# RMS norms of a two-block transformer kernel: the row factor applied after the matrix products instead of before

## The reference

```python
def rms_norm(x, gain):
    y = x * lax.rsqrt(jnp.mean(x * x, axis=-1, keepdims=True) + RMS_EPS)
    return y * gain
# first stack, layer i
x = x + mixer(rms_norm(x, norm_mix[i]), ...)
x = x + memory_cross_attention(rms_norm(x, norm_mem[i]), rms_norm(mem, norm_mem_src[i]), ...)
x = x + swiglu(rms_norm(x, norm_ffn[i]), ffn_w_in[i], ffn_w_out[i])
# second stack, layer l
h = _rmsnorm(x, g_mix[l]);  proj = h @ w_in[l]
gates = jax.nn.sigmoid(gate_pre + gate_b[l])       # 4 x 1024 columns of proj
x = x + jnp.sum(gates * branch, axis=2) @ w_out[l]
h = _rmsnorm(x, g_ffn[l])
u = _depthwise_conv(h @ w_up, conv_w, conv_b)      # 3 taps along the sequence
gate, up = jnp.split(u, 2, axis=-1)
x = x + (jax.nn.silu(gate) * up) @ w_down
```

## Time and profile before

| what | value |
|---|---|
| median of three runs | 1889.57 us |
| span of the profiled execution | 1888.8 us |
| PE busy | 1749.1 us, 93% |
| DVE busy | 1123.0 us, 59% |
| ACT busy | 822.7 us, 44% |
| POOL busy | 372.9 us, 20% |
| DMA share of 16 engines | 45.9%, mean 143 GB/s |
| mean granted TensorE clock | 0.948 |

### The profile page before, as it was taken

The page is one execution under the profiler, slowest core; times in us unless marked ns, Lnnn a source line. Parts: engine busy times, 40 slices in busy tenths (PEclk is TensorE's granted clock), DMA queues, the critical chain, the costliest instruction groups (busy, mean ns, idle before and its releaser), DMA issues. The chain is left out here.

```text
span 1888.8 us, 27948 instructions
## 1 busy us (share of the span) xinstructions
PE 1749.1 (93%) x11243; PEld 1575.8 (83%) x11243; DVE 1123.0 (59%) x1644; ACT 822.7 (44%) x1207; POOL 372.9 (20%) x462
## 2 busy tenths in 40 slices
PE   7899789999998988999989999899997999989998
PEld 6767679987886777899878799799976889979996
DVE  5757655544544655555446775677734676667763
ACT  4333344433342433444334446356524434636652
POOL 1500100001430000000014871201101595211100
PEclk9978899999977998999999999999998999999999
DMA  6401256656420023565465333566545534256654
GB/s 244 163 24 56 71 157 180 187 181 193 160 90 12 12 92 87 148 186 184 169 187 169 122 130 117 145 170 179 184 137 172 178 118 146 104 151 182 187 187 155
DMA packets 298695, 269.89 MB, mean 143 GB/s; under 512 B 19008, under 2 KB 258624, under 8 KB 298560
## 3 DMA queue, kind: packets, MB, share of 16 engines
q1 hardware_dynamic: 298560, 268.05, 45.9%
HBM read 266.97 MB, written 1.05 MB: 142 GB/s over the span
## 5 line engine op out<-in xcount | busy, mean ns | idle before, releaser
L139 DVE TENSOR_TENSOR w_lo<-w_raw,w_hi 128x2048 fp32r<-128x2048 f32 (+1 forms) x257 | 567.5, 2210 | 322.6 <-ACT w_hi L138 321.2
L138 ACT ACTIVATE w_hi<-w_raw 128x2048 fp32r<-128x2048 f32 (+1 forms) x257 | 468.6, 1826 | 195.5 <-PE bank L421 180.7
L1401 PE MATMUL bank<-mf_h_hi,w_hi 128*128 128x256 f32 x704 | 199.4, 283 | 0.0
L1401 PE MATMUL bank<-cffn_h_hi,w_hi 128*128 128x256 f32 x704 | 199.4, 283 | 0.0
L1403 PE MATMUL bank<-mf_h_hi,w_lo 128*128 128x256 f32 x704 | 199.2, 283 | 0.0
L1403 PE MATMUL bank<-cffn_h_hi,w_lo 128*128 128x256 f32 x704 | 199.2, 283 | 0.0
L1402 PE MATMUL bank<-mf_h_lo,w_hi 128*128 128x256 f32 x704 | 199.2, 283 | 0.0
L1402 PE MATMUL bank<-cffn_h_lo,w_hi 128*128 128x256 f32 x704 | 199.2, 283 | 0.0
L1401 PE MATMUL bank<-mix_h_hi,w_hi 128*128 128x256 f32 x576 | 166.9, 290 | 0.0
L1402 PE MATMUL bank<-mix_h_lo,w_hi 128*128 128x256 f32 x576 | 163.9, 284 | 0.0
L1403 PE MATMUL bank<-mix_h_hi,w_lo 128*128 128x256 f32 x576 | 163.8, 284 | 0.0
(11 more groups left out here) (518 smaller groups left out, 3736.4 us busy)
## 6 DMA issues: line engine op xcount, KB each, us to landing
w_raw<-in_w_in SPq DMA_DIRECT2D x50, 1024.0 KB, 5.1
w_raw<-in_ffn_w_in SPq DMA_DIRECT2D x88, 512.0 KB, 5.2
w_raw<-in_w_up SPq DMA_DIRECT2D x88, 512.0 KB, 5.0
w_raw<-in_ffn_w_out SPq DMA_DIRECT2D x20, 1024.0 KB, 4.9
w_raw<-in_w_down SPq DMA_DIRECT2D x20, 1024.0 KB, 5.0
w_raw<-in_nsa_w_in SPq DMA_DIRECT2D x10, 1024.0 KB, 5.1
w_raw<-in_ab_w_in SPq DMA_DIRECT2D x8, 1024.0 KB, 8.0
w_raw<-in_mem_w_kv SPq DMA_DIRECT2D x8, 1024.0 KB, 5.3
```

Source lines behind the costliest of these rows:

```text
L138: return act.activation(hi, raw, ACT.Copy)
L139: return dve.tensor_tensor(self.lo[:, cut_slot, 0:k * n], raw, hi.bitcast(F32), ALU.subtract)
L1401: pe.matmul(out, h, hi[:, f, :], start=(f == 0), stop=False)
```

## The change

The factor 1/rms leaves the path to the first product. `Norm` is replaced by `Features`: plain PE transposes of raw rows (L242 of the changed kernel), ACT and DVE multiply by the gain alone and split. Three things follow.

1. **Turning inside the residual.** `Residual` now has chunks of two k-rows throughout. Its last two chunks are worked bank by bank, in the order (rows 0, columns 0), (rows 1, columns 0), (rows 0, columns 1), (rows 1, columns 1). After each bank DVE adds it to `x_rows`, and four transposes of that quarter stand in PE's list one bank later; the last quarter follows the last bank. ACT and DVE round and cut features 0 to 3 there; features 4 to 7 follow in the next body.
2. **The factor later.** Where rows are on partitions it is the scale of the copies out of PSUM. Where features are on partitions (`stationary_job`) a row of factors is needed along the free axis: `RowFactors` spreads, turns and copies it, PE doing its part after job 0. DVE then multiplies each bank by it. In `block_conv_ffn` this gives a buffer `before`, and the taps are computed from it, the side taps one round of the loop later on DVE; `wide_lo` moves to POOL. In `block_branches` DVE copies out the 16 gate jobs in place of ACT, and ACT adds the bias in the sigmoids, 32 of 256 columns instead of 8 of 1024.
3. **The ring.** The loop of the second stack now has two chunks less, and `w.skip` leaves slots out so that each round begins at the same place: one cut slot after gate job 7, one raw and one cut slot before the four `mix_chunks`. A chunk behind a skipped cut slot waits for a later chunk to be used than before.

```diff
+class Features:
+    def turn(self, pe, t, half):
+        for f in range(4 * half, 4 * half + 4):
+            ins = pe.transpose(self.view(f)[:, t * P:(t + 1) * P], self.src[:, t, f * P:(f + 1) * P],
+                               self.k.ident[:, :])
+        ins.then_inc(self.turned, 1)
+    def round(self, act, features):
+        for f in features:
+            if not self.first:
+                act.wait_ge(self.turned, 2 * (f // 4) + 2)
+            act.activation(self.hi[:, f, :], self.view(f), ACT.Copy, scale=self.gain[:, f:f + 1])\
+               .then_inc(self.hi_done, 1)
...
+class RowFactors:
+    def dve(self, dve):
+        self.features.wait_factor(dve)
+        dve.tensor_copy(self.wide.rearrange("p (t q) -> p t q", q=P), free(self.features.rstd, [[1, T], [0, P]]))\
+           .then_inc(self.spread, 1)
+    def pe(self, pe):
+        pe.wait_ge(self.spread, 1)
...
@@ class Residual
+    ORDER = [(0, 0), (1, 0), (0, 1), (1, 1)]
+    TAIL = 2
...
+        for i, (t, half) in enumerate(self.ORDER):
...
+            if i < 3:
+                ins.then_inc(self.summed, 1)
+            if i and self.then is not None:
+                self.turn(pe, i - 1)
+        if self.then is not None:
+            self.turn(pe, 3)
+
+    def turn(self, pe, i):
+        pe.wait_ge(self.added, i + 1)
+        self.then.turn(pe, *self.ORDER[i])
...
@@ class Weights, round_to
-            if c >= self.CUT:
-                act.wait_ge(self.used, c - self.CUT + 1)
+            before = self.last_in(self.cut_slot, self.cut_slot(c), c)
+            if before is not None:
+                act.wait_ge(self.used, before + 1)
...
@@ block_branches
-        gate_chunks = [w.add(stationary_chunk(a["w_in_2"][layer], 6656, (2 * P * j,), 2 * P)) for j in range(16)]
+        gate_chunks = [w.add(stationary_chunk(a["w_in_2"][layer], 6656, (2 * P * j,), 2 * P)) for j in range(8)]
+        w.skip(0, 1)
+        gate_chunks += [w.add(stationary_chunk(a["w_in_2"][layer], 6656, (2 * P * j,), 2 * P)) for j in range(8, 16)]
...
+        w.skip(1, 1)
         mix_chunks = [w.add(stationary_chunk(a["w_branch_2"][layer], D, (2 * P * j,), 2 * P)) for j in range(4)]
...
                     w.round_to(act, gate_chunks[AHEAD + i] + 2)
                     if i == 12:
-                        act.wait_ge(gated, 2 * (AHEAD + 11))
+                        act.wait_ge(gated, AHEAD + 11)
                         for j in range(OPEN):
                             open_gates(act, j)
-                    gate(act, AHEAD + i)
...
                 def step(dve, i):
+                    if i:
+                        gate(dve, AHEAD + i - 1)
                     make_masks(dve, i)
...
@@ block_conv_ffn, scalar
                 for j in range(KF + 2):
                     if j < KF:
                         w.round_to(act, up[j] + 2)
-                        act.wait_ge(w.used, up[j] + 1)
+                        act.wait_ge(scaled, j + 1)
                         if j >= 2:
                             act.wait_ge(prod, j - 1)
...
                     if 1 <= j <= KF:
                         act.wait_ge(sides, 4 * j)
@@ block_conv_ffn, vector
-                for j in range(KF + 2):
+                for j in range(KF + 1):
                     if j < KF:
                         w.cut_to(dve, up[j] + 2)
-                        dve.wait_ge(middle, 2 * j + 2)
+                        dve.wait_ge(w.used, up[j] + 1)
+                        if j == 0:
+                            dve.wait_ge(row_factors.done, 1)
+                        dve.tensor_tensor(before[:, j % 2, :, :], k.bank[j % 4][:, :].rearrange("p (a q) -> p a q", q=S),
+                                          free(row_factors.rows, [[0, 2], [1, S]]), ALU.mult).then_inc(scaled, 1)
+                    if j >= 1:
+                        i = j - 1
+                        dve.wait_ge(middle, 2 * i + 2)
                         for side in range(2):
                             for half in range(2):
...
+                                u, v = before[:, i % 2, half, :], conv[:, i % 2, half, :]
```

More of the change, by code:

```diff
@@ new lines, in turn_all, with square @@
+    def turn_all(self, pe):
+        for half in range(2):
+            for t in range(T):
+                self.turn(pe, t, half)
+    def square(self, act, t, part):
+        n = D // self.parts
+        act.activation(self.scratch[t * self.parts + part], self.src[:, t, part * n:(part + 1) * n], ACT.Square,
+                       accum_out=self.stat[:, part, t:t + 1]).then_inc(self.squares, 1)
+    def round(self, act, features):
[4 more added lines that the diff above has]
+               .then_inc(self.hi_done, 1)
@@ L443, in act @@
             w.round_following(act)
+        if self.then is not None:
+            for i in range(2):
+                act.wait_ge(self.added, i + 1)
+                self.then.square(act, i, 0)
+            self.then.round(act, range(4))
+            if not self.final:
+                self.then.round(act, range(4, KD))
+                for t in range(T):
+                    act.wait_ge(self.added, 3 + t)
+                    self.then.square(act, t, 1)
     def dve(self, dve):
@@ L1086, in _ @@
                 project.act(act, squares)
-                mem.norm.act_round(act)
+                mem.features.round(act, range(KD))
                 mem.act(act, 0)
@@ L1125, in _ @@
                 project.dve(dve, sums)
-                mem.norm.dve_cut(dve)
+                mem.features.cut(dve, range(KD))
                 mem.dve(dve, 0)
@@ L1586, in _ @@
             def _(act):
-                norm.act_square(act)
+                rows.round(act, range(4, KD))
+                for t in range(T):
+                    rows.square(act, t, 1)
                 w.round_to(act, 1)
-                norm.act_round(act)
-                mem.norm.act_square(act)
+                mem.act_square(act)
                 def squares(act, j):
@@ L2185, in _ @@
                 cut(dve, 1)
+                for j in range(AHEAD):
+                    gate(dve, j)
                 turn.dve(dve)
```

561 lines of the change are left out of this document (303 added, 258 removed).

## The result

The changed kernel takes 1952.4 us (median of four runs, 1950.4 to 1955.8), the kernel before 1889.3 us in runs on the same chip. The ratio is 1.033, 95% interval 1.031 to 1.036: 63 us slower. The forecast was 1911 us, in a range from 1884 to 1945.

A forecast was written before the change was run, and what follows sets the result against it. PE was taken as the busy engine, its largest waits at the norms' turning. Terms -74 - 1.5 + 12.6 + 60 + 24 = +21 us on 1888.8 gave 1910, as a median 1911 us; range 1884 to 1945.

The forecast's parts named there:

- Gaps at the norms: Nine PE stops for turning rows by scaled identities: 103.8 us before, each gap now 2.8 us, gaining 74 us.
- the loop's jump: At the norms: the hardware loop's jump, no longer hidden under anything, adds 4.75 - 0.35 = 4.4 us once.
- What is late next: After the norms, outside convolution parts: PE waits for the second weight chunk and sometimes the factors' row, costing 12.6 us.
- Convolution loop: Convolution parts: DVE's new order makes ACT and DVE wait for each other, costing 30 us a layer, 60 in all.
- The circle: Convolution loop: closed chain of rounding, cut, multiplication, side taps and Silu, 7.04 us against PE's 5.76; bounds 6.6 and 7.8.
- Rival 1: Convolution loop: the circle does not bind, side taps hide, PE stays at 5.76 us a job; 1855 us, 13%.
- SwiGLU loop: SwiGLU parts: the chain between roundings takes 5.3 us, under PE's 5.76, and costs nothing.
- End of the mixing part: From gate job 14 to the first mixing product: the ring's skip delays it, 12 us a layer, 24 in all.
- End of the program: After PE's last product: the additions ended 4.0 us later, now 1.5 + 0.98 of transposes; gain 1.5 us.
- Rival 3: Convolution loop: side taps take 0.613 us each because GpSimd works beside them; 30 us more, 1941 us, 9%.
- Rival 4: Convolution loop: the clock falls as PE stands still 1.3 of 7 us; 36 us more, 1947 us, 6%.

## Why the prediction was wrong

- **Gaps at the norms, -74 us: right.** 2.6 us a gap against 2.8, and the loop's jump still costs PE 4.75 us. The run with late transposes shows, in the SwiGLU parts, that 2.3 us of a gap hang on their place.
- **"What is late next", +12.6 us: this step failed.** It named one successor, the second weight chunk, and stopped. It is right for the SwiGLU parts (-5.3 forecast, -5.9 and -5.3 measured). In the others the gain was real at the first product (in the first memory part it starts 1.0 us after the last addition, 200.53 against 199.49, where it was 8.5 us), but the end hung on chains that do not start at the first product: the keys' norm in DVE's queue, and in `nsa_` the load of the memory rows, issued 7.8 us after the body's first load. With them came the wait for the memory rows' low halves in `nsa_`. Against the forecast the memory parts lost 10 to 12 us and `nsa_` 9 to 10. Opening the first two gave 7.0 us (keys and `w_o`) and 7.3 or 7.9 us (the two edits in `nsa_`) in the medians of the whole kernel. The wait for the low halves was not opened by itself, and the rest of the memory parts' loss stays open. I had weighed no DMA of these parts, and of DVE's queue I had only written that the memory rows still wait for it, at no price, although both stood in the trace of before. That the residual's last chunks now have two k-rows, and so hold DVE 2.3 us instead of 1.2 in the memory attention, I had read as a matter of the ring alone.
- **Convolution loop, +60 us: right.** Each part came out 1.6 us above its forecast. The circle was forecast at 7.04 us and is 7.07, the multiplication 0.62 and is 0.6 from start to start, the side taps as the row with the PSUM operand had them. The order with the cut last shows the cost by itself: 59 us. Rival 1 falls. (The circle's upper bound should have read 7.9 us and not 7.8, by its own terms; nothing hangs on it.)
- **SwiGLU loop, 0: right.** PE is not held.
- **End of the mixing part, +24 us: right mechanism, too small.** Job 15 at +5.2 us (4.85 forecast), first mixing product at +25.6 (23.6). So 13.8 us a layer, not 12. The forecast for the whole part missed 7.6 us a layer. In the first round, roughly, 1.8 is that; 3.8 lie behind the first mixing product, where the first 21 matmuls run at 1.2 GHz (0.21 us apart instead of 0.12); 2.5 lie between the convolution jobs and gate job 14; the front is 0.4 better than forecast. Moving the skips gave back 10.9 and 10.2 us and shortened the time at the lower clock. I had priced each wait at its length and nothing for the clock that falls with it.
- **End of the program, -1.5 us: right.** The +0.8 of the table counts from the last addition, but the term counts from PE's last product. From its end at 1944.16 it is 6.9 us to the end of the span; before, from 1879.34, it was 9.4. With 0.7 us for the transposes inside the residual that is -1.8.
- **Rival 3** did not happen in the changed kernel (taps 0.49 us each), for the reason given: Silu comes last. It did happen once the order was changed, at 0.70 us. **Rival 4** did not happen in the convolution loop (0.99), but in the mixing part, where PE stood still for 4 us at a time.

What stays open is how much of the 3.8 and 2.5 us in the mixing part is the clock and how much DVE's and ACT's longer lists: no run here changed the clock alone. The same holds for the attention parts of the first stack.

## What to carry over

When a gap at the start of a part closes, list every chain in that part with the event that starts it (first product, body start, a DMA's issue, another engine's queue); the gain holds only where all of them start earlier. In a loop over two engines, follow one item around both lists and add the steps: if both engines wait for each other, it is the order that costs, and putting what nobody waits for last is free. A wait of a busy TensorE costs more than its length if the clock falls with it.

## What the hardware showed that I had not expected

- **DVE and GpSimd shut each other out.** Side taps (two SBUF inputs) took 0.48 us each alone; beside GpSimd's operations they took up to 0.98 us, 0.70 in the mean of 176. The other way round, GpSimd's 0.74 us operations took 2.27 us (product, cut last) and 2.78 us (`wide_lo`, product behind the taps) beside a DVE cut of 2.3 us, which itself did not slow down and had started first; GpSimd's operation ended 0.6 us behind it. The Trainium skill (SBUF — State Buffer, SBUF: two separate sides) describes an exclusive lock that whichever starts first holds for its whole instruction; the trace agrees, and so it is the order that decides who pays.
- **Issuing a DMA can take long itself.** Two loads of a small matrix in `nsa_` took SyncE 3.2 and 2.4 us to issue, and in the run with the memory rows first one took 6.8 us. What stands behind them in the list lands that much later. What makes them long is not shown.
- **Sixteen sigmoids of 256 columns take 6.49 us, four of 1024 took 3.90**, for the same number of elements: 0.41 against 0.98 us each.
